# A feed-forward up loop in Winograd form, its seven steps taken over a whole pair of tiles, with the weight sums formed on GpSimd; the branch mix in five column blocks

## The reference

```
hn = rms_norm(h); proj = hn @ w_in
mix = (gate_a * rwkv7_branch(proj) + gate_b * s5_branch(proj)) @ w_out     # s5: z = y @ w_glu; z[:, :D] * sigmoid(z[:, D:])
h = h + rms_norm(mix)
up = rms_norm(h) @ ffn_w_up                                                # 1024 -> 2 * 2816
a = causal_dwconv(up[:, :2816], conv_w, conv_b)                            # three taps along the tokens
f = (gelu(a) * up[:, 2816:]) @ ffn_w_down
h = h + rms_norm(f)
```

## Time and profile before

| | us |
|---|---|
| median of 3 runs | 3517.49 (3510.97 to 3517.65) |
| the profiled execution | 3515.69 |
| its span, first to last instruction | 3513.9 |
| busy in it: TensorE / VectorE / ScalarE / GpSimd | 3208.3 / 1823.9 / 1204.1 / 121.3 |
| mean granted clock of TensorE | 0.957 of full |
| matmuls of `branch_mix`, first to last | 1565.8 to 1844.6 |
| "mixout" | 1860.1 to about 2082 |
| `ffn_up`, first to last matmul | 2089.1 to 3014.4 |

### The profile page before, as it was taken

One profiled execution on the slowest core, in us unless ns is written; L12 is line 12 of the kernel. 1 busy time (PEld: TensorE's weight loads), 2 busy tenths in 40 slices (PEclk: granted clock), 3 DMA queues, 4 the chain that ended last, 5 costly groups with the idle time before them and its releaser, 6 DMA issues. The chain is left out here.

```text
span 3513.9 us, 70199 instructions
## 1 busy us (share of the span) xinstructions
PE 3208.3 (91%) x26794; PEld 2850.7 (81%) x26794; DVE 1823.9 (52%) x3270; ACT 1204.1 (34%) x1987; POOL 121.3 (3%) x126
## 2 busy tenths in 40 slices
PE   6999999999775888869998878999979999999998
PEld 6999999999754777759996757888858888788887
DVE  6566642222285566645434456766776776401433
ACT  5211123334373444442113334444443333311311
POOL 0000000000000222220000000000000000000000
PEclk8999999999887999979999989999989999999999
DMA  5233334333474334334326731221231222411432
GB/s 158 91 112 115 128 123 134 124 123 116 161 276 141 82 90 98 87 105 143 110 80 205 213 104 60 83 84 72 86 106 72 84 72 98 141 49 49 145 116 89
DMA packets 322659, 397.56 MB, mean 113 GB/s; under 512 B 134368, under 2 KB 263264, under 8 KB 311056
## 3 DMA queue, kind: packets, MB, share of 16 engines
q1 hardware_dynamic: 322576, 396.44, 35.7%
HBM read 252.97 MB, written 143.39 MB: 113 GB/s over the span
## 5 line engine op out<-in xcount | busy, mean ns | idle before, releaser
L434 PE MATMUL psum<-x_hi,proj_w_hi 128*128 128x344 f32 x1632 | 534.3, 327 | 4.4 <-DVE proj_w_lo L521 4.4
L434 PE MATMUL psum<-x_lo,proj_w_hi 128*128 128x344 f32 x1632 | 524.5, 321 | 0.0
L434 PE MATMUL psum<-x_hi,proj_w_lo 128*128 128x344 f32 x1632 | 523.3, 321 | 0.0
L2453 PE MATMUL psum<-up_x,up_w_hi 128*128 128x512 f32 (+2 forms) x1540 | 353.6, 352 | 57.4 <-ACT up_p L2479 50.5
L2459 PE MATMUL psum<-up_x,up_w_hi 128*128 128x512 f32 (+2 forms) x1540 | 352.1, 351 | 3.0 <-DVE up_x L2624 3.0
L2456 PE MATMUL psum<-up_x,up_w_lo 128*128 128x512 f32 (+2 forms) x1540 | 351.8, 351 | 0.0
L2453 PEld LDWEIGHTS psum<-up_x,up_w_hi 128*128 128x128 f32 x1540 | 259.5, 190 | 100.3 <-issue 52.7
L434 PEld LDWEIGHTS psum<-x_hi,proj_w_hi 128*128 128x128 f32 x1632 | 309.3, 190 | 5.8 <-issue 4.4
L434 PEld LDWEIGHTS psum<-x_lo,proj_w_hi 128*128 128x128 f32 x1632 | 309.0, 189 | 1.3
L434 PEld LDWEIGHTS psum<-x_hi,proj_w_lo 128*128 128x128 f32 x1632 | 308.7, 189 | 0.0
L2459 PEld LDWEIGHTS psum<-up_x,up_w_hi 128*128 128x128 f32 x1540 | 259.0, 189 | 44.2 <-DVE up_x L2624 3.5
(11 more groups left out here) (341 smaller groups left out, 5703.1 us busy)
## 6 DMA issues: line engine op xcount, KB each, us to landing
up_weight<-in_w_up_sets SPq DMA_DIRECT2D x44, 1024.0 KB, 5.0
scratch_hidden<-up_hidden SPq DMA_DIRECT2D x22, 1024.0 KB, 4.7
down_a_raw<-scratch_hidden SPq DMA_DIRECT2D x32, 704.0 KB, 6.2
proj_area<-scratch_s_tab SPq DMA_DIRECT2D x32, 608.5 KB, 3.8
scratch_s_tab<-proj_area SPq DMA_DIRECT2D x16, 1089.0 KB, 4.3
proj_weight<-in_w_in_tiles SPq DMA_DIRECT2D x34, 512.0 KB, 4.1
scratch_gates<-proj_mixed SPq DMA_DIRECT2D x16, 1032.0 KB, 4.0
chunk_pre<-scratch_roles SPq DMA_DIRECT2D x128, 128.0 KB, 2.7
```

The lines of the kernel that those rows point to most:

```text
L434: mm = nc.tensor.matmul(psum[:, bank(v, n), 0:N_TOK], w[:, v, k, :], x[:, k, cols], start=(k == 0 and w is w_hi and x is x_hi), stop=(k == ...
L2453: nc.tensor.matmul(out, w_hi[:, j, k, :], x_hi(phase, j)[:, k, cols], start=opens and k == 0, stop=False, skip_group_check=True)
```

## The change

In `branch_mix` the columns fall into 5 blocks of 416, 416, 416, 408 and 408 instead of 6 of 344; the two accumulators of the recurrent branch are banks 4 and 5, those of the S5 branch banks 0 to 3 (6 before); the buffer `term` is gone, the terms are formed in `sig`.

In "mixout" both parts of the first up weights (two loads of 1 MB) are issued where one was; the rows of the activation buffers are 516 elements apart (528 before), and the data begins 2 elements in.

In `ffn_up` the loop goes step by step: each of the seven products is made for all units of a pair before the next one. The order of the products is P_1, P_2, P_6, P_7, P_4, P_5, P_3. The 14 operands of a pair (q = 2 * step + part) go through the ring of 7 buffers; `high` and `low` of q + 7 stand behind step q. Sums and copies are written in place into `a_pre` and the new `b_pre`; P_5 and P_3 share an accumulator whose value after P_5 is added by VectorE before P_3 goes on. The weights' two halves (m1, m2) are loaded apart, 512 KB per part, the stores are per tile (512 KB), the gate product is one instruction per tile. In all pairs but the last of each pass GpSimd forms the eight weight sums of the next pair; the sums of the activations are on GpSimd too. The first set's sums and those of the pass's last pair stay on VectorE.

```diff
-        HALF = N_BLOCKS // 2
+        WIDTHS = (416, 416, 416, 408, 408)
...
-        A_BANKS, GLU_BANKS = 2, 6
+        A_BANKS, GLU_BANKS = 2, 4
...
-                                      ((up_weight[:, 0], ins["w_up_sets"][0, 0], first_set_loaded),)))
+                                      tuple((up_weight[:, part], ins["w_up_sets"][0, part], first_set_loaded) for part in range(2))))
...
 # ffn_up, SyncE
+            def pair(phase, m, first, last):
+                g = pair_of(phase, m)
+                final = last and phase == SECOND
+                after = 0 if last else m + 1
+                if not final:
+                    sp.wait_ge(w_lo_ready, 14 * g + 4)
+                    sp.wait_ge(t_ready, 8 * g + 8)
+                    load_m(0, after, m1_loaded)
...
+                if not (first and phase == FIRST):
+                    store(FIRST if first else phase, LAST if first else m - 1, 1, stored[1], g - 1)
...
+                if not final:
+                    sp.wait_ge(w_lo_ready, 14 * g + 14)
+                    load_m(1, after, m2_loaded)
+                store(phase, m, 0, stored[0], g)
 # ffn_up, TensorE
+            def pair(phase, m, first, last):
+                g, u0, n = pair_of(phase, m), units_before(phase, m), n_units(phase)
+                for step in range(7):
+                    for v, part, c0, c1 in units(phase):
+                        u, q = u0 + v, 2 * step + part
...
+                        freed, count = ((c21_done, u + 1 - n + 3), (c12_done, u + 1 - n + 3), (p1_copied, u + 1), (u2_copied, u + 1),
+                                        (u3_copied, u + 1), (c11_done, u + 1), (c22_done, u + 1))[step]
+                        out = psum[:, bank, 0:c1 - c0]
+                        pe.wait_ge(freed, count)
 # ffn_up, ScalarE
+                for q in range(14):
+                    step, part = q // 2, q % 2
+                    conv_free = lambda half: (conv_done[half], g + 1)
+                    b_free = lambda half: (b_used[half], g + 1)
+                    if step == P_1:
+                        copies(phase, m, step, part, first_half, conv_free(0) if part == 0 else b_free(0), p1_copied)
+                    if step == P_6:
+                        copies(phase, m, step, part, first_half, conv_free(1) if part == 0 else b_free(1), u2_copied)
+                    if step == P_7:
+                        copies(phase, m, step, part, second_half, conv_free(1) if part == 0 else b_free(1), u3_copied)
+                    if step == P_4:
+                        copies(phase, m, step, part, second_half, conv_free(0) if part == 0 else b_free(0), c21_done)
+                    if not (final and q >= 7):
+                        act.wait_ge(product_done[step], u0 + of_part(phase, part)[-1][0] + 1)
+                        high(g if q < 7 else g + 1, (q + 7) % 14)
+                    if q == 0 and not (first and phase == FIRST):
+                        gelu(g - 1, 1)
+                    if q == 10:
+                        gelu(g, 0)
 # ffn_up, GpSimd
+            def sums_12(g, part):
...
+                    pool.wait_ge(m1_loaded[part], 16 * g)
+                    pool.wait_ge(m2_loaded[part], 16 * g)
+                    pool.wait_ge(w_hi_ready, 14 * g)
+                    pool.wait_ge(w_lo_ready, 14 * g)
+                b11, b21, t2, b12, t4, t1, b22 = (weight_of(part, step) for step in range(7))
+                G.tensor_tensor(t1, b12, b11, ALU.subtract).then_inc(t_ready, 1)
+                pool.wait_ge(t_ready, 8 * g + 2 * part + 1)
+                G.tensor_tensor(t2, b22, t1, ALU.subtract).then_inc(t_ready, 1)
+            def sums_34(g, part):
...
+                G.tensor_tensor(b12, b22, b12, ALU.subtract).then_inc(t_ready, 1)
+                G.tensor_tensor(t4, b21, t2, ALU.subtract).then_inc(t_ready, 1)
+            def pair(phase, m, first, last):
+                g = pair_of(phase, m)
+                if last and phase == FIRST:
+                    for op in (O_S3, O_S1, O_S2, O_S4):
+                        x_sum(SECOND, op)
+                elif not last:
+                    for part in range(2):
+                        sums_12(g + 1, part)
+                    for part in range(2):
+                        sums_34(g + 1, part)
 # ffn_up, VectorE
+                for q in range(14):
+                    step, part = q // 2, q % 2
+                    if step == P_2:
+                        added(phase, m, step, part, first_half, 0, p1_copied, c11_done)
+                    if step == P_5:
+                        added(phase, m, step, part, second_half, 1, u3_copied, c22_done)
+                    if step == P_3:
+                        added(phase, m, step, part, first_half, 1, u2_copied, c12_done)
+                    if not (final and q >= 7):
+                        low(g if q < 7 else g + 1, (q + 7) % 14)
+                    if q == 1 and not (first and phase == FIRST):
+                        gated(g - 1, 1, u0)
+                    if q == 9:
+                        conv(phase, m, 0)
+                        if last and phase == FIRST:
+                            sums_12(g + 1, 0)
+                    if q == 10 and last and phase == FIRST:
+                        sums_12(g + 1, 1)
+                    if q == 11:
+                        gated(g, 0, u0 + n_units(phase))
+                        if last and phase == FIRST:
+                            sums_34(g + 1, 0)
+                            sums_34(g + 1, 1)
+                    if q == 12:
+                        conv(phase, m, 1)
...
+                    if last and phase == FIRST and q == 13:
+                        x_low(SECOND, O_A11)
+                    if first and phase == SECOND:
+                        for at, op in ((1, O_A12), (3, O_S2), (5, O_S3), (6, O_A22), (7, O_S1), (8, O_S4)):
+                            if q == at:
+                                x_low(SECOND, op)
```

More of the change, by code:

```diff
@@ L1790, in branch_mix @@
         LAST = KD // 2 - 1
-        HALF = N_BLOCKS // 2
+        WIDTHS = (416, 416, 416, 408, 408)
+        NB = len(WIDTHS)
+        STARTS = [sum(WIDTHS[:n]) for n in range(NB)]
+        HALF = NB // 2
         place_first = lambda x: x.rearrange("p (a c) -> p a c", a=S5_CHUNK)
@@ L2350, in ffn_up @@
         block = ctx.enter_context(nc.Block())
         FF_PAIRS, LAST = M_FF // 2, M_FF // 2 - 1
-        EDGE = CONV_W - 1
         FIRST, SECOND = range(2)
         REST = 16 * (UP_COLS // P)
-        A11, A21, A22, A12 = range(4)
-        RAW_AT = {FIRST: 0, SECOND: 4}
-        PLACE = {FIRST: (2, 3, 5, 4, 0, 1, 6), SECOND: (5, 4, 1, 0, 2, 3, 6)}
-        OP_A11, OP_A12, OP_S2, OP_S1, OP_S3, OP_S4, OP_A22 = range(7)
-        P_1, P_2, P_6, P_5, P_7, P_3, P_4 = range(7)
-        x_hi = lambda phase, op: x_space[2 * PLACE[phase][op]]
@@ new lines, in ffn_up @@
+        A11, A21, A12, A22 = range(4)
+        O_A11, O_A12, O_S2, O_S3, O_A22, O_S1, O_S4 = range(7)
+        P_1, P_2, P_6, P_7, P_4, P_5, P_3 = range(7)
+        RAW_AT = {FIRST: (12, 10, 13, 9), SECOND: (0, 1, 2, 3)}
+        HI_AT = {FIRST: (0, 2, 4, 6, 8, 10, 13), SECOND: (1, 8, 9, 10, 11, 12, 13)}
+        LO_AT = {FIRST: (1, 3, 5, 7, 9, 11, 12), SECOND: (0, 2, 5, 6, 3, 4, 7)}
+        QUARTER = {O_A11: A11, O_A12: A12, O_A22: A22}
+        x_hi = lambda phase, op: x_space[HI_AT[phase][op]]
@@ L2490, in x_high @@
             def x_high(phase, op):
-                n = width_of(phase)
-                last_units = units_before(SECOND, 0)
                 if phase == SECOND:
-                    quarter = {OP_A11: A11, OP_A12: A12, OP_A22: A22}.get(op)
-                    if quarter is not None:
-                        act.wait_ge(rest_loaded[quarter], REST)
-                    held = {OP_A11: P_6, OP_A12: P_5, OP_S2: P_3, OP_S1: P_7, OP_A22: P_4}.get(op)
+                    if op in QUARTER:
+                        act.wait_ge(rest_loaded[QUARTER[op]], REST)
@@ new lines, in x_high, with copies @@
+                nc.scalar.activation(x_hi(phase, op)[:, :, used(phase)], source_of(phase, op)[:, :, used(phase)], ACT.Copy).then_inc(x_hi_ready[op], 1)
+            def copies(phase, m, step, part, into, free, copied):
+                for v, _, c0, c1 in of_part(phase, part):
+                    act.wait_ge(product_done[step], units_before(phase, m) + v + 1)
+                    act.wait_ge(*free)
+                    late = into is second_half
+                    s0 = max(c0, EDGE) if late else c0
+                    half = {P_1: 0, P_6: 1, P_7: 1, P_4: 0}[step]
+                    nc.scalar.activation(into(part, half, s0, c1), psum[:, a_bank(v), s0 - c0:c1 - c0], ACT.Copy).then_inc(copied, 1)
@@ L2573, in _ @@
             V = nc.vector
[L2574 to L2582 removed]
+            for half in range(2):
+                dve.sem_inc(b_used[half], 1)
+                dve.sem_inc(conv_done[half], 1)
@@ new lines, in low, with x_low @@
+            def low(g, q):
+                step, part = q // 2, q % 2
```

(19 more changed lines are left out.)

637 lines of the change are left out of this document (276 added, 361 removed).

## The result

| | before | after |
|---|---|---|
| median of 4 runs, us | 3516.86 (3510.97 to 3517.65) | 3669.57 (3668.18 to 3670.25) |
| profiled execution, us | 3515.69 | 3670.25 |
| its span, us | 3513.9 | 3668.5 |
| mean granted clock of TensorE | 0.957 | 0.941 |

The changed kernel is slower: the ratio is 1.0437, 95% interval 1.0419 to 1.0456. The forecast was 3637, its own range 3595 to 3665, so the time lies just above the forecast's own range and within the range for eight in ten.

A forecast was written before the change was run, and what follows sets the result against it. TensorE was taken to bound the steady part, ScalarE's and VectorE's splits the start and middle. Terms -4 + 4 - 6 - 5.5 + 107 + 18 + 3 + 3.5 = +120 gave 3637 us; eight-in-ten range 3518 to 3675.

The forecast's parts named there:

- branch_mix: `branch_mix` stage: 1728 matmuls become 1440, 13 ns each; -4 us taken, bounds -8 and +3.
- mixout: "mixout": activations queue behind a second megabyte of weights; +4 us, bounds 0 and +8.
- pair 0, with its share of wait and clock: Start of the up loop: splits now stand between steps, -6 us; with its wait and clock, +0.1.
- 18 steady pairs: nine 0.61s: Steady pairs of the up loop: nine TensorE waits of 0.61 for ScalarE's copies vanish, -5.5 us.
- 18 steady pairs: P_3's wait: Steady pairs: P_3 waits for VectorE's addition behind `conv`, 5.2 or 5.5 us a pair; +96.3 here, +107 in twenty pairs.
- 18 steady pairs: clock: Steady pairs: some 8 matmuls slower after the wait, 1.7 us, half taken; +16.2 here, +18 in all.
- passage, with its share of wait and clock: Between the two passes of the up loop: 107 us against 104, +3; with its wait and clock, +9.4.
- last pair to "down": End of the up loop: taps, gelu and a larger gate product delay the last store; +3.5 us.
- the turns: VectorE and GpSimd alternate instructions on SBUF; four sums stretch `conv` of tile 0, 4.25 us extra a pair.
- Rival (c): Slower still: the clock falls in every pair and sums hold back low parts; 3685 us, chance 0.08.
- Rival (a): One GpSimd sum gets in, not four; waits of 2.85 and 3.2 us a pair, 3573 us, chance 0.20.
- Rival (b): The engines do not meet, or GpSimd's sums end in time; waits 0.95 and 1.3 us, 3510.5 us, chance 0.15.

The follow-up runs named there:

- e8: The kernel before with only the new `branch_mix` (five column blocks); 3512.6 us, ratio 0.9989.
- e3: The changed kernel, with GpSimd's eight weight sums of a pair waiting until `conv` of tile 0 is done; 3582.3 us, ratio 1.0176.
- e2: The changed kernel, with VectorE's `conv` of tile 0 after both additions of P_5, its gelu and gate product two places later; 3528.5 us, ratio 1.0029.
- e4: The changed kernel with weight sums on VectorE in every pair and `conv` of tile 0 after both additions of P_5; 3526.9 us, ratio 1.0025.
- e5: e4's kernel with activation sums on VectorE too, no GpSimd in the up loop; very last pair's `conv` of tile 0 back ahead of the additions; 3517.9 us.
- e7: The changed kernel, with GpSimd copying one operand of each weight sum instead of forming it (steady pairs' sums left out); 3571.4 us in one run.
- e1: The changed kernel, with the weight sums of every pair on VectorE and GpSimd only summing activations; 3587.3 us, ratio 1.0200.

## Why the prediction was right, and where it was not

Step by step, on the span, which grew by 154.6:

| step | forecast | measured | by what |
|---|---|---|---|
| branch_mix | -4 | -4.6 | 289.7 against 294.3; alone in e8 the same |
| mixout | +4 | +4.3 | first matmul of the stage to that of the up loop: 233.2 against 229.0; the stall 13.37 |
| pair 0, with its share of wait and clock | +0.1 | +0.7 | 69.9 against 69.2 |
| 18 steady pairs: nine 0.61s | -5.5 | -5.5 | no wait for a copy is left |
| 18 steady pairs: P_3's wait | +96.3 | +88.3 | 4.6 and 5.2 a pair, forecast 5.2 and 5.5 |
| 18 steady pairs: clock | +16.2 | +46.5 | 129.3 longer in all, less the waits; some 43 of it clock, the rest the step order |
| passage, with its share of wait and clock | +9.4 | +21.8 | 126.1 against 104.3 |
| last pair to "down" | +3.5 | +3.7 | the wait for its weights 10.57, before 7.2 |

The measured time lies 5 us above the forecast's own range, so the direction and the mechanism came out, and the size was too small by 33.

**The mechanism** was the one forecast: the addition behind `conv`, and the turns. The forecast's parts are confirmed one by one: the order alone costs 1.17 and 0.81 (e3; forecast 1.3 and 0.95), the turns the rest (e3 against after), and neither costs P_3 anything once the addition stands ahead (e2). The 160 sums have means of 1394 to 1975 ns, all above 1270; the second and third tap of a tile take 1.67 us each on the mean in seven pairs of SECOND, against 1.285; the row of the third:

```profile
L2725 DVE SCALAR_TENSOR_TENSOR up_hidden<-up_a_pre,cols_sb,up_hidden 128x1024 f32<-128x1024 f32 x14 | 23.4, 1668 | 2.1 <-DVE up_hidden L2723 2.1
```

The bound from two SBUF inputs was carried over to the taps and the small copy from the earlier trace rows, which shows neither; it held for both. By the Trainium skill (SBUF — State Buffer, section on SBUF's two separate sides) VectorE takes the shared ports in a two-port mode too, not with two SBUF inputs alone. The trace agrees with that as far as it goes: the first tap and the edge copy read one tile of SBUF each and were held (0.81 became 1.59, 0.16 became 1.26), while additions out of PSUM kept their 0.68; in which mode an instruction ran, no row shows.

**The step that failed is the size of the clock term.** The prediction said "some 8 matmuls cost 0.2 more each, 1.7, where the clock falls", and then took half because it was unsure that the clock would fall. It fell in every pair, and 7 to 15 matmuls of 512 columns were slow (11.7 on the mean of the nine steady pairs of SECOND): 85.7 us of full work at 0.50 in the 18 pairs, which costs 43, or 2.4 a pair. The other 3.6 of the 46.5 are not clock; e2 and e4, with no wait and a clock of 1.00, are as much above the old pairs (5 us in 18 pairs). Rival (c) had the clock in every pair, but at 1.7. In the passage the waits are 34.5 us in all, which is what the prediction's single waits (13, 8, 8, 5.5) add up to; in part that is luck, as they were 13.5, 4.7, 7.6 and 8.6. The pairs took 12 more than that forecast because TensorE came out of these waits at the low clock: 24.5 us of full work at 0.50, 5.4 before; length less waits is 91.6 in the two pairs, 81.0 before. Over the whole loop the waits grew by 93 us where the terms for them come to 102, and the busy time by 62 where the clock term was 18.

**Rival (a)**, one sum getting in, fails on the timeline: four sums come in, as in the forecast; a pause of 0.15 before a tap is enough. **Rival (b)**, the engines not meeting, fails on the same rows. What it would have given is not shown by one run: e3 has its waits at P_3 (0.81 and 1.17; it named 0.95 and 1.3) but a second wait behind them, and e5, with no GpSimd instruction in the loop, has `conv` late; it took 3517.9, where (b) had 3510.5.

**What the prediction did not ask** is whether `conv` has to stand ahead of the additions. It gave the order's cost (20 waits) and took the order as given; another order took 141 of the 153 us away with GpSimd's sums still there. The turns were needed as well: with no sums beside `conv` of tile 0, the old place cost 87 us less (e3).

## What to carry to other kernels

Look at what stands in the same engine's list ahead of the instruction that the bottleneck waits for, and put the long work that nobody waits for behind it; that took 141 us off here, while who formed the weight sums decided nothing measurable once it was done. Work moved from VectorE to GpSimd is not taken off VectorE while both use SBUF: a chain of dependent VectorE instructions loses a whole GpSimd instruction at each pause, so short work for GpSimd, placed where VectorE has slack, or none. Price a wait of TensorE of about 5 us at half as much again for the clock behind it (2.4 behind 4.9 on the mean here).

## What the runs showed of the hardware that I had not expected

**The clock behind a wait.** After waits of 4.5 to 5.6 us the granted clock was 0.50 for 3.0 to 6.1 us of full work. After waits of 0.8 to 1.6 it stayed at 1.00 (e3, and e7 in FIRST). After waits of 1.9 to 2.5 it did both (e1, e3, e7), and after one of 3.69 it fell (e3). In e7 two waits of P_3, 2.10 and 2.03 long, in pairs of the same shape; the window behind the first, and the windows behind the second:

```profile
2770.80:2776.40 5.60, 5.60 (x24) 4.57 (x25) 4.93 (x8) 1.37 (x3) 0.00 (x0) 1.00 0.35 113
```
```profile
2813.00:2814.00 1.00, 1.00 (x5) 0.85 (x4) 1.00 (x3) 0.01 (x1) 0.00 (x0) 0.87 0.00 0
2814.00:2815.00 1.00, 1.00 (x4) 0.71 (x4) 0.92 (x1) 0.00 (x0) 0.00 (x0) 0.50 0.00 0
...
2816.00:2817.00 1.00, 1.00 (x4) 0.80 (x3) 0.53 (x1) 0.45 (x1) 0.00 (x0) 0.50 0.99 397
```

The second pair took 43.0 us, the first 41.5; the clock fell some 1.5 us after the wait had ended, when TensorE was at work again. In e1 pairs with a wait of 2.14 took 42.2 or 43.7. So a wait of this size costs itself or itself and 1.5 us; what decides between the two, the runs do not show. By the Trainium skill (TensorE: Matmul & The Clock Gate, Part 1) the low clock is the state of rest, and activity lifts it. The rows agree that it comes back under work (above, behind 6 and 3 us of it); the fall itself can come when TensorE is at work again, 1.5 us after the wait in the rows here.

**A turn can be long.** A VectorE instruction of 0.68 us lasted 4.99 beside a GpSimd sum of 2048 elements (e4), and an edge copy of two elements 1.26 instead of 0.16 (the changed kernel).

**Still open.** With no wait and a clock of 1.00 a pair of SECOND takes 39.2 to 39.4 in the step order, 38.9 in the old one, for the same 168 matmuls; a unit of 512 columns takes 2.78 to 2.81 (e2), in e4 up to 2.93, where it took 2.78. The alternation of the accumulators, the rows 516 elements apart and the other transfers beside it were not told apart.
